# Stages around an mLSTM and two joined scans in a two-block network: norm adds on GpSimd, scalings and squares on ScalarE, channel rows in tiles of 128, row stores spread over their stages

## The reference, cut to what matters

```python
# layer 1 of the first block: mLSTM mixer (4 heads of 192 channels, ML_W = 768)
h = x @ w_in;  xm, z, gates, q_mem = split(h, [768, 1536, 1552])
xc = silu(conv5(xm) + conv_b)                  # over tokens, per channel
q = xc_h @ w_qkv[0];  k = (xc_h @ w_qkv[1]) * 192**-0.5;  v = xm_h @ w_qkv[2]   # per head
g = gates + gate_b                             # 16 gate columns
hs = normalise_per_head(mlstm(q, k, v, g) + mlstm_reversed(q, k, v, g)) * norm_g
y = (hs + skip * xc) * silu(z);  mixed = concat(y, memory_attention(q_mem, mem_k, mem_v))
# both layers of the first block
x = layer_norm(ALPHA * x + mixed @ w_out);  x = layer_norm(ALPHA * x + moe(x))  # 16 experts, top 2
# second block, even mixer: a gated delta rule (4 heads of 128) and an RWKV-7 scan (8 heads of 64),
# each forward and backward, the two directions added, normalised per head, gated; last layer: out = x + embedding
```

## Time and profile before

| what | value |
|---|---|
| median of 3 runs | 5903.64 us (5903.53 to 5908.01) |
| profiled execution, its own time | 5902.24 us |
| its span, first to last instruction | 5900.4 us |
| TensorE busy | 4985.5 us, 84% of the span |
| VectorE, ScalarE, GpSimd busy | 40%, 20%, 11% |
| stretch 1353 to 1707 us (mLSTM inputs) | PE 346.4 busy of 354, granted clock 0.95 |
| stretch 1951 to 2063 us (mLSTM output) | DVE 80.1 busy of 112, ACT 50.8, PE 58.5 |
| stretch 3408 to 4136 us (joined scans) | PE 678.1 busy of 728, DVE 442.4 |
| stretch 4140 to 4214 us (even mixer's output) | DVE 55.8 busy of 74, ACT 25.0 |
| stretch 5888 to 5900 us (end) | no engine busy, DMA 350 GB/s |

### The profile page before, as it was taken

How to read it: one execution, slowest core, us unless ns; L and a number is a source line. 1 busy time by engine, 2 the same in 40 slices (tenths; PEclk the granted TensorE clock), 3 DMA queues, 4 the chain that set the end, 5 groups by cost and what they waited for, 6 DMA issues and landing times. The chain is left out here.

```text
span 5900.4 us, 97463 instructions
## 1 busy us (share of the span) xinstructions
PE 4985.5 (84%) x40401; PEld 2637.2 (45%) x40401; DVE 2376.1 (40%) x3825; ACT 1195.4 (20%) x2176; POOL 627.2 (11%) x481
## 2 busy tenths in 40 slices
PE   7998779868988576996889989999499998967698
PEld 5554323224457432322333479999244443312243
DVE  2345520023126662002634756666643532533341
ACT  1223101012212310101422312222211213411111
POOL 0000100010000040001220000000221332311100
PEclk9999889988989787998899999999799999988899
DMA  4111286662335427675332342332501223667620
GB/s 154 51 51 47 85 302 216 249 243 61 104 102 153 150 86 302 241 276 206 88 96 81 121 98 63 75 70 47 221 29 50 82 89 141 212 234 277 227 84 34
DMA packets 579796, 810.57 MB, mean 137 GB/s; under 512 B 174368, under 2 KB 333600, under 8 KB 578920
## 3 DMA queue, kind: packets, MB, share of 16 engines
q1 hardware_dynamic: 515480, 638.54, 32.8%
q0 software_dynamic: 26240, 95.43, 4.7%
q10 hardware_dynamic: 37712, 71.35, 3.3%
HBM read 1366.67 MB, written 199.82 MB: 265 GB/s over the span
## 5 line engine op out<-in xcount | busy, mean ns | idle before, releaser
L158 PE MATMUL ri_acc<-xT,ri_w 128*128 128x512 f32 (+1 forms) x576 | 254.4, 601 | 12.0 <-DMA ri_w<-in_even_w_in 12.0
L648 PE MATMUL na_acc<-xT,na_w 128*128 128x512 f32 x448 | 215.4, 628 | 14.7 <-ACT na_q L716 7.0
L158 PE MATMUL mi_acc<-xT,mi_w 128*96 128x512 f32 (+1 forms) x512 | 223.3, 596 | 0.0
L4480 PE MATMUL le_gp<-le_g,xT 128*128 128x512 f32 x512 | 220.9, 592 | 0.0
L158 PEld LDWEIGHTS ri_acc<-xT,ri_w 128*128 128x128 f32 (+1 forms) x576 | 109.0, 191 | 157.2 <-issue 145.0
L213 PE MATMUL hi_acc<-hi_T,hi_S 128*128 128x512 f32 x384 | 170.0, 592 | 0.0
L780 DVE SCALAR_TENSOR_TENSOR na_e<-na_s,na_bs 128x256 f32<-128x256 f32 (+1 forms) x96 | 47.1, 491 | 292.1 <-PE na_t L674 253.1
L1757 PE MATMUL moe1e_y_ps<-moe1e_wd,moe1e_hT 128*32 128x512 f32 x1280 | 149.4, 609 | 13.9 <-DMA moe1e_wd<-in_exp_w_down 9.3
L1757 PE MATMUL moe0e_y_ps<-moe0e_wd,moe0e_hT 128*32 128x512 f32 x1280 | 149.0, 608 | 14.0 <-DMA moe0e_wd<-in_exp_w_down 11.9
L1736 PE MATMUL moe0e_u_ps<-moe0w_wu,moe0e_xb 128*32 128x512 f32 x1280 | 144.4, 604 | 18.1 <-DMA moe0w_wu<-in_exp_w_up 9.1
L1840 DVE TENSOR_TENSOR moe0e_hy<-moe0e_hy,moe0e_u_ps 128x512 f32<-128x512 f32 x20 | 13.7, 687 | 352.7 <-ACT moe0e_hy L1806 352.7
(11 more groups left out here) (780 smaller groups left out, 9788.6 us busy)
## 6 DMA issues: line engine op xcount, KB each, us to landing
moe0w_wu<-in_exp_w_up SPq DMA_DIRECT2D x80, 2048.0 KB
xT<-in_exp_w_gate SPq DMA_DIRECT2D x80, 2048.0 KB
x_tm<-in_exp_w_gate SPq DMA_DIRECT2D x80, 2048.0 KB
moe0e_wd<-in_exp_w_down SPq DMA_DIRECT2D x80, 2048.0 KB
moe1w_wu<-in_exp_w_up SPq DMA_DIRECT2D x80, 2048.0 KB
moe1e_wd<-in_exp_w_down SPq DMA_DIRECT2D x80, 2048.0 KB
scratch_rk_f<-ri_out POOLq DMA_DIRECT2D x8, 2048.0 KB, 7.0
sc_rx<-scratch_rk_f SPq DMA_DIRECT2D x32, 512.0 KB, 4.8
```

The costliest lines, as they stand in the source:

```text
L158: mm = pe.matmul(self.acc[i % 2][0:n, h * BANK:(h + 1) * BANK], self.wbuf[i % 3][:, k, 0:n], self.rhs[:, k, h * BANK:(h + 1) * BANK], star ...
L648: mm = pe.matmul(acc[:, h * BANK:(h + 1) * BANK], wt[:, u, :], xT[:, u, h * BANK:(h + 1) * BANK], start=(u == 0), stop=(u == KD - 1))
L4480: mm = pe.matmul(gp[:, n % 2, h * BANK:(h + 1) * BANK], xT[:, k, n * P:(n + 1) * P], g[:, k, h * BANK:(h + 1) * BANK], start=(k == 0), sto ...
```

## The change

1. `mlstm_inputs`: tiles of 128 channel rows (14 product tiles). Gate logits with the weights stationary in four column quarters, then eight small matmuls that add the quarters. A head of 192 channels is a full tile and half a tile; two neighbouring heads share their half tiles, whose matmuls use the upper and the lower half of the array (rows or columns). Outputs go through a ring of four PSUM banks and four SBUF slots, k and v by token in one store per head. The factor of k goes into its weights once, on VectorE.
2. `mlstm_out`: the add of the directions goes to GpSimd; of two heads' scalings in a memory step one goes to ScalarE; six channel rows of 128.
3. `two_scans`: the two loops around L3544 are exchanged.
4. `even_out`: the delta rule's add goes to GpSimd, its squares to ScalarE with a sum for each head (no reduce), its scaling to ScalarE (32 copies with a scale); the gates' Silu starts within the tile loop; one gate load moves ahead in SP's queue.
5. Experts: token rows are stored tile by tile in the projection stage, as they are normed; first gate before first up; two down weights load in routing; in layer 0 the first up weight loads in the projection stage; at the end the token rows' load moves ahead of the last down weights.
6. The last stage stores each result tile as it is added; `transfer` goes.

```diff
 class MemorySteps:
-            link(dve.reciprocal(self.rs[:, b, :], self.rs[:, b, :]))
-            for h in range(2):
+            dve.reciprocal(self.rs[:, b, :], self.rs[:, b, :]).then_inc(self.inverted, 1)
+            dve.wait_ge(self.inverted, k + 1)
+            for h in range(self.heads_of_dve):          # 1 in mlstm_out
...
+            act.wait_ge(self.inverted, k + 1)
+            act.activation(self.e[:, k % 3, self.M:], self.e[:, k % 3, self.M:], ACT.Copy,
+                           scale=self.rs[:, k % 3, 1:2]).then_inc(self.probs_by_act, 1)
 def project_pairs_and_norm:
+                    for n in range(NT):
+                        sp.wait_ge(normed, n + 1)
+                        sp.dma_start(x_rows[n * P:(n + 1) * P], x_tm[:, n, :]).then_inc(rows_stored, 16)
 def route:
-                sp.dma_start(x_rows.rearrange("(n p) d -> p n d", p=P), x_tm[:]).then_inc(x_stored, 16)
-                early.load_up(sp, 0, 0)
+                early.load_gate(sp, 0, 0)
+                if not early.up_is_there:
+                    early.load_up(sp, 0, 0)
                 early.load_up(sp, BACKWARD, E - 1)
                 sp.wait_ge(halves, T // BANK)
                 early.load_gate(sp, BACKWARD, E - 1)
-                sp.wait_ge(x_stored, 16)
-                early.load_gate(sp, 0, 0)
+                early.load_down(sp, 0, 0)
+                early.load_down(sp, BACKWARD, E - 1)
 def expert_blocks:
-                next_down(TURNS - 1, None, 0, even)
                 sp.wait_ge(gates, 2 * TURNS)
                 sp.dma_start(x_tm[:], x_rows.rearrange("(n p) d -> p n d", p=P)).then_inc(x_back, 16)
+                next_down(TURNS - 1, None, 0, even)
 def mlstm_inputs:                                       # two heads (even, odd), 512 columns
+                    pe.matmul(a, even[:, 0:P], x[:, 0, :], start=True, stop=False)
+                    pe.matmul(b, odd[:, 0:P], x[:, 2, :], start=True, stop=False)
+                    pe.matmul(a, rest[low, 0:P], x[low, 1, :], start=False, stop=True)
+                    pe.matmul(b, rest[high, 0:P], x[high, 1, :], start=False, stop=True).then_inc(extra, 1)
+                    free(k + 2)
+                    pe.matmul(both[low], even[:, P:DH], x[:, 0, :], start=True, stop=False)
+                    pe.matmul(both[high], odd[:, P:DH], x[:, 2, :], start=True, stop=False)
+                    pe.matmul(both[low], rest[low, P:DH], x[low, 1, :], start=False, stop=True)
+                    pe.matmul(both[high], rest[high, P:DH], x[high, 1, :], start=False, stop=True).then_inc(extra, 1)
                                                         # k and v by token
+                    for a in range(2):
+                        free(k + a)
+                        for m in range(2):
+                            pe.matmul(out[a][m], src[m][:, 2 * a, :], wf[:, 1 + m, 2 * pair + a, :], start=(m == 0), stop=False,
+                                      skip_group_check=True)
+                    for m in range(2):
+                        for a, r in enumerate((low, high)):
+                            mm = pe.matmul(out[a][m], src[m][r, 1, :], wp[r, 1 + m, pair, :], start=False, stop=True, skip_group_check=True)
 def mlstm_out:                                          # GpSimd; even_out has the like for its da, db
+                for n in range(NT):
+                    pool.wait_ge(tile_loaded[n % 4], 32 * (n // 4 + 1))
+                    pool.tensor_tensor(a[:, n, :], a[:, n, :], b[:, n % 4, :], ALU.add).then_inc(summed, 1)
 def two_scans:
-                    for d in range(2):
-                        for h in range(HEADS):
+                    for h in range(HEADS):
+                        for d in range(2):
                             mm = pe.matmul(s_out[d][:, h, :], kts[c][half[d], h, :], vn[half[d], h, :], start=True, stop=True)
 def even_out:                                           # ScalarE, in the tile loop
+                    for h in range(dn_heads):
+                        c = slice(h * DD, (h + 1) * DD)
+                        act.activation(sq[:, 0, 0, c], da[:, n, c], ACT.Square, accum_out=var[:, n, h:h + 1]).then_inc(dn_squares, 1)
...
+                    for h in range(dn_heads):
+                        c = slice(h * DD, (h + 1) * DD)
+                        act.activation(da[:, n, c], da[:, n, c], ACT.Copy, scale=rstd[:, n, h:h + 1]).then_inc(scaled, 1)
 def layer_embedding:
+                        sp.wait_ge(added, n + 1)
+                        sp.dma_start(out[n * P:(n + 1) * P], x_tm[:, n, :]).then_inc(out_stored, 16)
```

More of the change, by code:

```diff
@@ L283, in combine @@
         dve.tensor_tensor(out, self.acc[0:n, (Y, W, V, X)[j], :], self.part[0:n, (0, 2, 3, 1)[j], :], ALU.add).then_inc(self.combined, 1)
-def transfer(nc, name, pairs):
-    with Stage(nc, name) as s:
-        done = s.sem("done")
-        with s.block() as block:
-            @block.sync
-            def _(sp):
-                for dst, src in pairs:
-                    sp.dma_start(dst, src).then_inc(done, 16)
-                sp.wait_ge(done, 16 * len(pairs))
 class Chain:
@@ new lines, in gate_logits @@
+                def gate_logits():
+                    pe.wait_ge(wg_loaded, 16)
+                    pe.wait_ge(zeros, 1)
+                    for hf in range(T // BANK):
+                        half = slice(hf * BANK, (hf + 1) * BANK)
+                        for k in range(KD):
+                            part = slice(k % 4 * QUARTER, (k % 4 + 1) * QUARTER)
+                            mm = pe.matmul(lp[part, hf, :], wgate[:, k, :], xT[:, k, half], start=(k < 4), stop=(k >= KD - 4))
+                        mm.then_inc(halves, 1)
@@ new lines, in free, with by_feature @@
+                def free(use):
+                    if use >= RING:
+                        pe.wait_ge(copied, use - RING + 1)
+                def by_feature(u):
+                    _, pair, which, half = u
+                    k = ring.first[u]
+                    a, b, both = (ep[:, (k + j) % RING, :] for j in range(3))
+                    x = xc[:, 3 * pair:3 * pair + 3, half * BANK:(half + 1) * BANK]
+                    even, odd = wf[:, which, 2 * pair, :], wf[:, which, 2 * pair + 1, :]
+                    rest = wp[:, which, pair, :]
+                    pe.wait_ge(silu, 3 * pair + 3)
+                    free(k)
+                    pe.matmul(a, even[:, 0:P], x[:, 0, :], start=True, stop=False)
+                    free(k + 1)
+                    pe.matmul(b, odd[:, 0:P], x[:, 2, :], start=True, stop=False)
[6 more added lines that the diff above has]
+                    pe.matmul(both[high], rest[high, P:DH], x[high, 1, :], start=False, stop=True).then_inc(extra, 1)
@@ L1981, in _ @@
[L1981 to L1993 removed]
+                        gate_rows()
@@ L1999, in _, with keep_extra @@
-                act.wait_ge(g_exp, 1)
-                act.activation(lf[:], lf[:], ACT.Ln, bias=1.0).then_inc(g_ln, 1)
+                def keep_extra(u):
+                    k = ring.first[u]
+                    feature = u[0] == "f"
+                    width = BANK if feature else 2 * DH
+                    for j in range(3 if feature else 2):
+                        if (k + j) >= RING:
+                            act.wait_ge(stored[(k + j) % RING], ring.stored_before(k + j))
+                        act.wait_ge(extra, ring.groups[u] + (2 if j == 2 else 1))
+                        act.activation(eo[:, (k + j) % RING, 0:width], ep[:, (k + j) % RING, 0:width], ACT.Copy).then_inc(copied, 1)
@@ L2001, in _ @@
+                for hf in range(T // BANK):
+                    act.wait_ge(halves, hf + 1)
+                    act.activation(quarters[:, hf * BANK:(hf + 1) * BANK], lp[:, hf, :], ACT.Copy).then_inc(halves_kept, 1)
                 act.wait_ge(c_loaded, 32)
```

420 lines of the change are left out of this document (241 added, 179 removed).

## The result

| | median | lowest to highest | runs |
|---|---|---|---|
| before, same chip | 5905.83 us | 5903.53 to 5909.30 | 4 |
| changed kernel | 5826.84 us | 5823.41 to 5833.16 | 4 |

A forecast was written before the change was run, and what follows sets the result against it. TensorE, busy 84% of the span, was taken as the main bound, with other engines or stores filling some stages. Inputs -73, scans -9, mLSTM output -15, even output 0, experts -9, end -9, semaphores +1: -114, forecast 5789 us; range 5764 less 4 to 5816.

The forecast's parts named there:

- The experts' -9: Expert stages: -3 in the first, -6 in the second, 0 at their ends; -9 us, from -18 to +5.
- The -6: Second expert stage: shorter TensorE waits for the first gather and a gate weight, -6 us (0 to -10).
- the third rival: Experts give nothing or lose, as down loads and row load push weights TensorE needs: about 5800 us, chance 0.10.
- The scans' -9: Joined scans: exchanged loops take L3544 from 1.71 to 1.09 us a step, -9 us (0 to -10).
- TensorE runs into it without idle time: Joined scans, L3544: reason given for counting the line's saving of 0.61 x 16 = 9.8 us as on the path.
- The ring of four: mLSTM inputs: output slots costed at nothing, covered by a 13.9 us product tile; otherwise each burst would show 5 us.
- The rule weighed in the prediction: mLSTM inputs: tiling-mode changes drain the array, 0.156 us each; units 80 us, stage -66, total 5796, chance 0.08.
- the row's 72: mLSTM inputs: by-feature and by-token units at 72.4 us in all, from a Hyena convolution row of half-array instructions.
- The 9 for the loop: mLSTM output, token loop: 9 us gained of the 13.3 that VectorE loses over eight periods.
- The 6 for two rows less: mLSTM output, channel rows: six rows in place of eight save 5 to 10 us, taken as 6.
- The 0.7 per tile added for contention: Even mixer's output: VectorE's two operations on pairs of tensors slowed beside GpSimd's add, 0.7 us a tile.
- the first rival: Array halves don't overlap: mLSTM inputs give only -43 us and the scans nothing, total 5828, chance 0.06.

The follow-up runs named there:

- e9: Changed kernel with its whole expert part undone, five rounds: 5828.72 us, ratio 0.9874.
- e11: Changed kernel run again with no edit, five rounds: 5828.73 us, ratio 0.9875.
- e1: Kernel before with only the exchanged loops around the state products of the joined scans: 5905.23 us.
- e6: Changed kernel with the mLSTM output's add on VectorE again and the scans' old loop order: 5827.61 us.
- e7: Changed kernel with both heads' scalings of the mLSTM output on VectorE again: 5831.09 us.
- e3: Changed kernel with the by-feature half-array matmuls of the inputs issued out of pairs and the scans' old loop order: 5857.22 us.
- K = 128: Changed kernel with 128 semaphore increments that nobody waits for on TensorE ahead of the joined scans, five rounds: 5815.08 us, ratio 0.9842.

## Why the prediction was wrong, point by point

1. **The experts' -9 failed as a step.** The prediction took away the 4 MB of token rows, and let the two down loads count only against the first stage's gather. They came ahead of the gather in both, so the DMA engines were as full beside the second one as before (share 1.04 at either; its wait 11.3 before, 11.4 after). The -6 taken from the second stage's gather and gate together came to 0 and some 2, and the row load that moved ahead, costed at 0, put off the last weights by 3.1 us in the first stage and 0.7 in the second. Net 0: e9 equals e11. This is the mechanism of the third rival, given 0.10.
2. **The scans' -9 was right for the work and wrong for the time.** TensorE's busy time falls by 9.4 us (678.1 to 668.7), and e1 shows the same 9.5. Then "issue" grows by 6.7 in the profiled pair and by 9.9 in e11, nearly all of it where TensorE's blocks of 256 instructions come late, which begin elsewhere in the step. The step that failed is "TensorE runs into it without idle time": it looked at the idle time ahead of L3544 and not at what the idle time elsewhere hangs on. Through it -9 became -3 in this pair; over the eight profiles with the changed kernel's scans the stage is 728.3 to 734.4, 731.7 in the mean against 732.4 before.
3. **Inputs: mechanism right, 5.6 short.** 278.06 us busy against 275.0: units of 4.94 by feature in the mean (forecast 4.55) and 2.31 by token (2.25), 76.5 in all for 72.4, less 1.1 at the product tiles and the gates. In the unit shown the four full matmuls take 1508.88 - 1507.07 = 1.81 us (forecast 4 x 0.436 = 1.74) and the six pairs 3.08 (12 x 0.234 = 2.81). Another 1 us is the start, where the gate weights gave 1 in place of 2, and 2.0 the stage's end, from TensorE's last matmul to the next stage (10.8 before, 12.8 after); 0.4 is the rounding of 73.4 to 73. The ring of four never shows: no wait of TensorE in the stage after the first.
   The rule weighed in the prediction, that a change of mode drains the array (the Trainium skill, TensorEngine Tiling (Array Packing), Key Properties), holds in part: the units' 76.5 us lie between the row's 72 and the rule's 80.
4. **mLSTM output: -13.3 for -15, near by two errors that cancel.** The 9 for the loop measured 4.8: from the stage's start to VectorE's first operation on a channel row it is 77.9 us before and 73.1 after. The 6 for two rows less measured 8.1: from that operation to the end of the last row 30.5 and 22.4 us. The first rows' starts and the last rows' ends, before and after:

```profile
2029.21 1.28 DVE L2517 SCALAR_TENSOR_TENSOR mln_o<-mln_mscore,mln_par,mln_ex 96x1024 f32<-96x1024 f32 x1 [3.26 <-ACT mln_ga L2458]
...
2058.45 1.22 DVE L2520 TENSOR_TENSOR mln_o<-mln_o,mln_ga 96x1024 f32<-96x1024 f32 x1
```

```profile
1964.14 1.28 DVE L2626 SCALAR_TENSOR_TENSOR mln_o<-mln_mscore,mln_par,mln_ex 128x1024 f32<-128x1024 f32 x1 [3.26 <-ACT mln_ga L2569]
...
1985.27 1.23 DVE L2629 TENSOR_TENSOR mln_o<-mln_o,mln_ga 128x1024 f32<-128x1024 f32 x1
```

   The period of 5.21 beats the 5.9 that was named, since GpSimd's adds took 1.80 us each (forecast 1.9 to 4.8) and were over 15 us after the first began. In that stretch VectorE's scalings stood behind the adds: the first statistics come 2.4 us later in the stage than before, and the first period is 2.6 longer than the 6.97 of the old loop. The 2.5 and 7.2 of e6 and e7 are what undoing one part costs, and don't add up to the loop's gain: in e7 the scalings put back stand behind the adds too.
   The Trainium skill, GPSIMD Engine Reference, Key points, says that GpSimd shares its SBUF interfaces with VectorE, and that VectorE's instructions in a 2-port mode or with two SBUF inputs contend with it. The trace agrees for the two inputs, with 1.115 us for 0.684 in the even output; the scalings, which read one tensor, contend as well, 1.88 us for 0.35, and no run here tells in which mode they run.
5. **Even output +0.9 for 0, end -9.4 for -9:** as forecast. The 0.7 per tile added for contention was 0.43 + 0.22 (1.115 and 0.910 for 0.684 and 0.692). The squares taken at 0.36 were 0.29 and 0.19 more for the read of each sum, which the prediction left out; the scalings of 11.6 were 9.5. The +1 for more semaphores to clear stands on no row: no run shows it, and the execution's time exceeds its span by 1.8 us in both kernels.
6. **What stays open.** Of the 37 us between forecast and profiled difference, 13 lie in the experts' stages, 6 in the scans, 6 in the inputs, 2 in the mLSTM output, 1 in the even one and 10 in the other stages, most of which the change doesn't touch; of these the means of the several profiles leave 2, so some 8 us of the profiled pair's shortfall is scatter. The total of 5827 lies on the first rival's 5828 by coincidence: its condition is false (e3). Of the 13, 3 to 4 are a first expert stage that is 533.4 us in e11 and 533.3 in e9 against 529.0 to 531.1 in three profiles of the old program: longer without the expert edits too (one profile), and not explained. Nor is the mean of +1.7 in the untouched mLSTM scan, nor why the recurring gap of L2816 differs between programs (4 to 14 us). That a shift also lowers the busy time (668.7 to 664.5 with K = 128) wasn't followed up.

## What to carry to other kernels

Bytes taken out of a queue help only if nothing takes their place ahead of the load that is waited for: list what the DMA engines hold at that moment, before and after. In a long stage of small matmuls written out instruction by instruction, an edit anywhere ahead can move some 10 us by moving where blocks of 256 instructions begin, so a small change there is judged by busy time and by "issue" apart, and a few instructions of no work in a wait that hides them are worth trying. Half-array matmuls pair by their order of issue alone, which here was worth 25 us.

## What the runs showed of the hardware

- TensorE's irregular gaps in the scans, 0.15 to 1.7 us each, lie 256 instructions apart, or multiples of that, and come to between 4.5 and 17 us of 700 in the table above, by where the blocks begin. Each block comes in one packet of 16.4 KB (0.9 to 1.9 us in the changed kernel), which begins only after the place ahead of that block is passed.
- An increment of a semaphore on TensorE takes 0.15 us: from K = 128 to 192, where the wait no longer hides them, 64 of them put off the first matmul by 9.8 us.
- A scaling on VectorE that begins during a GpSimd add of two tensors ends with that add: 0.15 us behind it for 256 columns (1.88 us in place of 0.35), 0.03 for 2 columns (up to 1.63 in place of 0.17). Operations on two tensors of 512 columns in the even output end 0.55 us behind it (up to 1.78 in place of 0.68). The maximum, at 0.68, and the statistics, at 0.35, run on beside the adds.
- Each sum that ScalarE accumulates beside its output costs a read of 186 ns of its own.
- Two matmuls on separate halves of the array start 0.01 us apart, and the pairs 0.48 to 0.54 us behind each other, where full ones of as many columns go at 0.43 to 0.48.
